# A gated delta rule whose triangular inverse is turned in 32x32 blocks by VectorE, with narrower merge products and K*S in place of W

## The reference

```python
m = jnp.where(strict, jnp.einsum('bhnid,bhnjd->bhnij', kb, k) * decay, 0.0)
t_inv = lax.linalg.triangular_solve(eye + m, ..., lower=True, unit_diagonal=True)
u = jnp.einsum('bhnij,bhnjd->bhnid', t_inv, v * beta[..., None])
w = jnp.einsum('bhnij,bhnjd->bhnid', t_inv, kb * jnp.exp(gc)[..., None])
...
    v_new = u_n - jnp.einsum('bhck,bhkv->bhcv', w_n, state)
    o_n = (jnp.einsum('bhck,bhkv->bhcv', qg_n, state)
           + jnp.einsum('bhij,bhjv->bhiv', qk_n, v_new))
    state = state * jnp.exp(gl_n)[..., None, None] + jnp.einsum('bhck,bhcv->bhkv', kd_n, v_new)
```

## Time and profile before

| | us |
|---|---|
| median of three runs | 3276.89 |
| span of the profiled execution, first to last instruction | 3272.8 |
| TensorE busy (PE) | 3167.1 (97%) |
| VectorE busy (DVE) | 2267.4 (69%) |
| ScalarE busy (ACT) | 1691.8 (52%) |
| GpSimd busy (POOL) | 821.7 (25%) |

### The profile page before, as it was taken

How to read it: one execution, slowest core, us unless ns; L and a number is a source line. 1 busy time by engine, 2 the same in 40 slices (tenths; PEclk the granted TensorE clock), 3 DMA queues, 4 the chain that set the end, 5 groups by cost and what they waited for, 6 DMA issues and landing times.

```text
span 3272.8 us, 62859 instructions
## 1 busy us (share of the span) xinstructions
PE 3167.1 (97%) x19574; PEld 2770.4 (85%) x19574; DVE 2267.4 (69%) x4218; ACT 1691.8 (52%) x3583; POOL 821.7 (25%) x1372
## 2 busy tenths in 40 slices
PE   5999999999989999999999998999999999999998
PEld 4989898989878888888888887888888888888887
DVE  5777777777756588667886767875667645775566
ACT  5565656565644455444555555324555444454444
POOL 1000000000010189888888830661000000000000
PEclk8999999999999999999999999999999999999999
DMA  6444444444447777777777876886666676666754
GB/s 163 120 123 110 129 107 128 112 121 119 116 132 182 202 200 208 210 201 207 200 203 202 209 194 179 239 243 171 181 188 186 179 188 185 180 183 177 182 152 141
DMA packets 1047697, 560.62 MB, mean 171 GB/s; under 512 B 47664, under 2 KB 1035472, under 8 KB 1047104
## 3 DMA queue, kind: packets, MB, share of 16 engines
q1 hardware_dynamic: 980608, 495.38, 56.7%
q10 hardware_dynamic: 58160, 37.63, 4.0%
q0 software_dynamic: 8848, 26.59, 2.6%
HBM read 530.40 MB, written 29.13 MB: 171 GB/s over the span
## 4 chain that ended last, share of the span: by engine, by line
PE 79%; DVE 9%; DMA 4%; issue 4%; ACT 3%; SPq 1%; ACTq 1%; DVEq 0%; POOL 0%; POOLq 0%
PE bank L293 44%; PE bank L294 22%; PE bank L637 5%; DVE w_lo L281 4%; DMA u_scratch<-u 3%; ACT w_hi L275 1%; DVE tiles L1929 1%; DVE normed L1941 1%; PE bank L635 1%; DVE tiles L308 1%; SPq L477 1%; PE bank L698 1%; PE bank L711 0%; PE bank L600 0%; PE bank L751 0%
## 5 line engine op out<-in xcount | busy, mean ns | idle before, releaser
L293 PE MATMUL bank<-act,w_hi 128*128 128x512 f32 x4352 | 1586.3, 406 | 19.6 <-DVE act L330 8.1
L281 DVE TENSOR_TENSOR w_lo<-raw,w_hi 128x512 fp32r<-128x512 f32 x1856 | 1308.2, 755 | 190.6 <-ACT w_hi L275 177.7
L294 PE MATMUL bank<-act,w_lo 128*128 128x256 f32 x4352 | 1217.5, 280 | 0.0
L293 PE MATMUL bank<-mid,w_hi 128*128 128x512 f32 x3072 | 1096.0, 401 | 21.8 <-DVE mid L1943 13.9
L275 ACT ACTIVATE w_hi<-raw 128x512 fp32r<-128x512 f32 x1856 | 1040.2, 621 | 87.1 <-PE bank L294 64.5
L293 PEld LDWEIGHTS bank<-act,w_hi 128*128 128x128 f32 x4352 | 819.8, 188 | 213.5 <-DVE w_lo L281 13.4
L294 PE MATMUL bank<-mid,w_lo 128*128 128x256 f32 x3072 | 865.8, 282 | 0.0
L294 PEld LDWEIGHTS bank<-act,w_lo 128*128 128x128 f32 x4352 | 823.0, 189 | 5.0 <-issue 4.1
L293 PEld LDWEIGHTS bank<-mid,w_hi 128*128 128x128 f32 x3072 | 583.0, 190 | 165.8 <-DVE mid L1943 15.1
L294 PEld LDWEIGHTS bank<-mid,w_lo 128*128 128x128 f32 x3072 | 586.3, 191 | 0.0
L303 ACT ACTIVATE tiles<-bank 128x256 f32<-128x256 f32 x384 | 146.3, 381 | 597.4 <-PE bank L294 593.2
(11 more groups left out here) (325 smaller groups left out, 2945.4 us busy)
## 6 DMA issues: line engine op xcount, KB each, us to landing
raw<-in_mlp_w_up_dram SPq DMA_DIRECT2D x128, 1024.0 KB, 6.4
raw<-in_mlp_w_down_dram SPq DMA_DIRECT2D x128, 1024.0 KB, 6.1
raw<-in_gdn_w_in_dram SPq DMA_DIRECT2D x96, 1024.0 KB, 5.9
raw<-in_gdn_w_out_dram SPq DMA_DIRECT2D x32, 1024.0 KB, 6.5
raw<-in_ple_w_gate_dram SPq DMA_DIRECT2D x32, 1024.0 KB, 6.1
raw<-in_s_w_out_dram SPq DMA_DIRECT2D x28, 1024.0 KB, 6.8
raw<-in_s_w_in_dram ACTq DMA_DIRECT2D x10, 1024.0 KB, 12.6
c_scratch<-c_pow ACTq DMA_DIRECT2D x32, 256.0 KB, 4.4
```

Of the source, the lines that this page charges most:

```text
L281: eng.tensor_tensor(w_lo[par][:, c], raw[slot][:, c], w_hi[par][:, c].bitcast(F32), ALU.subtract).then_inc(S("lo_ready"), 1)
L293: eng.matmul(a[:, :], w_hi[par][:, w], rhs[:, k0 + kt, :], start=(k0 + kt == 0), stop=False)
L294: mm = eng.matmul(a[:, 0:NT], w_lo[par][:, w], rhs[:, k0 + kt, 0:NT], start=False, stop=(k0 + kt == kend - 1))
```

## The change

- VectorE turns Pm, P2, P4 and (in place of all three turns of RT) R, by its transpose of 32x32 blocks; R and the powers are block-diagonal there in blocks of 16 or 32. After the second merge only one 32x32 corner of each half is turned anew. TensorE's turns of Pm and RT and its products for P2T and P4T go, with ScalarE's copies of them.
- P2 is made in slot 0, P4 in slot 1, P8 in slot 2; the products with R follow one slot earlier too, and the first form of R is needed in slot 1.
- The second merge multiplies Mp itself (no L2) by the second half of each pair of columns, 64 moving columns with 96 stationary ones; the third has 64 stationary ones and full 128 rows. ScalarE writes the new columns of RT.
- W and nW go. Vb of block 1 gets minus beta*exp(gc) times K*S added to it (the sign sits in column H_BEXP), by two VectorE operations in slot 12; K*S is one product with 256 columns.
- The state follows one slot earlier. `decays(r+1)` moves from slot 13 to slot 15, ahead of `squares(r+1)`; `scalars(r+1)` moves behind the new operations of slot 12; the slot's `split_lo` goes last there. The rest of VectorE's side work is split in `before` and `after` the core.

TensorE and ScalarE:

```diff
                 if s == 0:
                     w("P_ready")
-                    four(A, Pm, None, "PT_turned", True)
+                    w("PT_ready")
+                    four(C, PT, Pm, "power_done")
                 elif s == 1:
-                    w("power_out", 4, 1)
-                    four(C, PT, Pm, "power_done")
-                    four(F, Pm, PT, "power_done")
-                elif s == 2:
-                    w("power_out", 4, 2)
+                    w("power_out", 3, 1)
                     w("RT_ready", 7, 1)
                     four(A, P2, RT, "R_done")
                     w("transposed_out", 2, 1)
                     four(C, P2T, P2, "power_done")
-                    four(F, P2, P2T, "power_done")
...
+                elif s == 6:
+                    w("RT_ready", 7, 5)
+                    for m in range(4):
+                        mm = pe.matmul(A[0:96, 64 * m:64 * m + 64], Mp[:, m, 0:96], second_half(RT, m), start=True, stop=True)
+                    mm.then_inc(S("X_done"), 1)
                 elif s == 7:
...
+                    for m in range(4):
+                        mm = pe.matmul(C[0:96, 64 * m:64 * m + 64], Dm[:, m, 0:96], packed(WT, m), start=True, stop=True)
...
+                        mm = pe.matmul(A[0:64, 64 * m:64 * m + 64], Mp[:, m, 0:64], RT[:, m, 64:128], start=True, stop=True)
...
+                elif s == 12:
+                    w("sides_ready", 3, 3)
+                    pe.matmul(F[:, 0:NT], kq[:, 1, 1, :], state[:, :, :].rearrange("p h v -> p (h v)"), start=True,
+                              stop=True).then_inc(S("chunk_done"), 1)
                 elif s == 13:
-                    w("sides_ready", 5, 5)
-                    w("sides_ready", 5, 4)
+                    w("Vb_less")
                     for hd in range(2):
-                        dst = A[:, (2 + hd) * P:(3 + hd) * P]
-                        pe.matmul(dst, RT[:, 2 + hd, :], Vb[:, 2 + hd, :], start=True, stop=False)
-                        mm = pe.matmul(dst, nW[:, hd, :], state[:, hd, :], start=False, stop=True)
+                        mm = pe.matmul(A[:, (2 + hd) * P:(3 + hd) * P], RT[:, 2 + hd, :], Vb[:, 2 + hd, :], start=True, stop=True)
...
                 elif s == 13:
-                    decays(r + 1)
                     gate_tanh(n + 6, 0, y[:, 1, :], "conv_done", 4 * r + 6)
                 elif s == 15:
+                    decays(r + 1)
                     squares(r + 1, n + 7)
```

VectorE:

```diff
+                ve.wait_ge(S("P_ready"), r + 1)
+                ve.transpose(fl(PT), fl(Pm)).then_inc(S("PT_ready"), 1)
...
+                if s == 0:
+                    w("power_out", 3, 1)
+                    ve.transpose(fl(P2T), fl(P2)).then_inc(S("transposed_out"), 1)
+                elif s == 1:
+                    add_to_R(1)
+                    w("power_out", 3, 2)
+                    ve.transpose(fl(P4T), fl(P4)).then_inc(S("transposed_out"), 1)
...
+                    add_to_R(3)
+                    w("RT_ready", 7, 4)
+                    ve.transpose(fl(Dm), fl(RT)).then_inc(S("Dm_ready"), 1)
+                elif s == 5:
+                    w("R_done", 6, 4)
+                    w("RT_ready", 7, 4)
+                    TT(fl(RT), fl(RT), C[:, :], ALU.subtract).then_inc(S("RT_ready"), 1)
+                    w("RT_ready", 7, 5)
+                    ve.transpose(fl(Dm), fl(RT)).then_inc(S("Dm_ready"), 1)
+                elif s == 7:
+                    w("RT_ready", 7, 6)
+                    ve.transpose(Dm[32:64, :, 0:32], RT[0:32, :, 32:64]).then_inc(S("Dm_ready"), 1)
...
+                elif s == 12:
+                    w("chunk_done", 5, 3)
+                    w("sides_ready", 3, 2)
+                    for hd in range(2):
+                        last_ = STT(Vb[:, 2 + hd, :], F[:, hd * P:(hd + 1) * P], hs[:, H_BEXP + hd:H_BEXP + hd + 1],
+                                    Vb[:, 2 + hd, :], ALU.mult, ALU.add)
+                    last_.then_inc(S("Vb_less"), 1)
...
-            def around(r, s, last):
+            def before(r, s, last):
 
                 n = 6 * r
-                if s == 1:
+                if s == 0:
+                    ve.wait_ge(S("PT_ready"), r + 1)
+                    TT(RT[:, :, :], PT[:, :, :], ident.unsqueeze(1).to_broadcast([P, 4, P]), ALU.add).then_inc(S("RT_ready"), 1)
+                elif s == 1:
```

More of the change, by code:

```diff
@@ L667, in core @@
                     mm.then_inc(S("qk_done"), 1)
-                elif s == 4:
-                    w("power_out", 4, 4)
+                elif s == 3:
+                    w("power_out", 3, 3)
                     w("RT_ready", 7, 3)
@@ L672, in core @@
                     w("o_log")
-                    for b in range(2):
-                        mm = pe.transpose(E[:, b * P:(b + 1) * P], kq[:, 1, b, :], ident)
-                    mm.then_inc(S("kv_turned"), 1)
-                elif s == 5:
[L677 to L681, removed]
+                    pe.transpose(E[:, 0:P], kq[:, 1, 0, :], ident).then_inc(S("kv_turned"), 1)
+                elif s == 4:
+                    w("RT_ready", 7, 4)
+                    w("L_ready")
+                    four(A, L1, RT, "X_done")
+                elif s == 5:
                     w("Dm_ready", 3, 1)
@@ L718, in core @@
                     mm.then_inc(S("chunk_done"), 1)
[L719 to L723, removed]
+                elif s == 11:
                     w("VN_ready", 2, 1)
-                    w("sides_ready", 5, 2)
                     for hd in range(2):
@@ L1200, in head @@
                             split_hi(se, 6 * r + m, q, m % 3, 2 * r + m // 3 + 1, par=m % 2)
-                    if s in (0, 4, 12, 16, 20):
-                        around(r, s, last)
-                        core(r, s)
-                    else:
-                        core(r, s)
-                        around(r, s, last)
+                    around(r, s, last)
+                    core(r, s)
                     if s == 17:
@@ L1908, in around, with after @@
                     key_matrix(r + 1)
+            def after(r, s):
+                if s == 12:
+                    ve.wait_ge(S("Vb_less"), r + 1)
+                    ve.wait_ge(S("sides_ready"), 3 * r + 3)
+                    scalars(r + 1)
                 elif s == 22:
-                    conv(r + 1, n + 8, 2)
+                    conv(r + 1, 6 * r + 8, 2)
             def head(r, last):
                 for s in range(24):
-                    if s < 8 or not last:
-                        m = 5 + s // 4
-                        split_lo(ve, 6 * r + m, s % 4, 0 if last and m == 6 else m % 3, m % 2)
+                    split = s < 8 or not last
+                    m = 5 + s // 4
+                    quarter = lambda: split_lo(ve, 6 * r + m, s % 4, 0 if last and m == 6 else m % 3, m % 2)
+                    if split and s != 12:
+                        quarter()
                     if s == 19 and not last:
                         unit_qk(r + 1)
+                    before(r, s, last)
                     core(r, s)
-                    around(r, s, last)
+                    if not last:
+                        after(r, s)
+                    if split and s == 12:
+                        quarter()
             with ve.Fori(0, KH - 1) as r:
```

125 lines of the change are left out of this document (44 added, 81 removed).

## The result

| | before | after |
|---|---|---|
| median of 20 runs each, us | 3275.82 (3264.72 to 3293.38) | 3286.97 (3279.82 to 3294.78) |
| span of the profiled execution, us | 3272.8 | 3284.2 |
| TensorE busy, us | 3167.1 | 3113.2 |
| start of the last slot 14, us | 942.56 | 952.38 |

A forecast was written before the change was run, and what follows sets the result against it. TensorE, without idle time in the heads, was taken as the bound. A head of 23.24 + 24.02 + 5.0 + 1.84 = 54.1 us gave -18.2 us in all, lost clock +10, so 3268 us; range 3238 to 3298.

The forecast's parts named there:

- S14 to S1: TensorE's slot 14 to next slot 1 core starts: moved decays and Pm's transpose lengthen R's chain; 23.24 us, 2.9 waiting.
- S11 to S13: TensorE's slot 11 to 13 core starts: VectorE adds K times state to Vb first; 5.0 us, 0.9 waiting.
- S13 to S14: TensorE's slot 13 to 14 core starts: 1.84 us, VectorE reaching the VN copy with some 0.3 to spare.
- S1 to S11: TensorE's slot 1 to 11 core starts: fewer turns and products, narrower weights; 24.02 us, where before it was 29.53.
- I take the share of the loads: Narrow weights on TensorE: a 0.89 us group falls to 0.51 with 64 stationary columns, 0.70 with 96.
- Hidden edits: Other transposed powers, L2's mask, R's transposes, ScalarE's dropped turned copies and the weights' DMA: nothing waited for changes.
- The bounds: Head length for narrow weights gaining nothing to full proportion, and transpose price one to two copies: 53.8 to 55.9 us.
- The clock: Gap at slot 1 drops TensorE's clock to half for 3.4 us: 1.4 us in half of 14 heads, +10 us.
- The ends: Outside the 14 full periods: head 0, with no chain before it, saves 4.3 us; the last one loses 0.8.
- TensorE did not stay the bound: Rival: slack hides both lengthened chains, a head is 49.2 us; 3185 us, chance 0.16 including halfway cases.
- the clock did not hold: Rival: same lengthened chains but no clock loss from the gaps; -18.2 us, 3259 us, chance 0.22.
- it was not lost for longer: Rival: behind slot 1 the clock halves for 6.8 us or falls twice, 2.8 us a head; 3298 us, chance 0.17.

The follow-up runs named there:

- Both experiments on the decays: Changed kernel with decays(r+1) back in ScalarE's slot 13: 3260.7 us, ratio 0.9949; kernel before with decays(r+1) moved to slot 15: 3297.8 us, 1.0065.
- the wide kernel: Changed kernel with all 128 stationary columns in the narrow groups of slots 6 to 9, same moving columns: 3294.7 us, ratio 1.0076 to the kernel before.
- the second scheduling edit: ScalarE's four Vb copies moved from slot 8 to 9, on the changed kernel with decays already back in slot 13: 3260.1 us, ratio 0.9956 to before.
- the Vb copies alone: Changed kernel with only ScalarE's four Vb copies moved from slot 8 to slot 9: 3285.3 us, ratio 1.0033 to the kernel before.
- Nine and four fillers: Unread products in slot 1 ahead of the waits, on the changed kernel with decays and Vb copies moved: nine 3245.7 us (0.9919), four 3239.7 us (0.9889).

## Why the prediction was wrong

Between the spans the change made +11.4 us; the steps gave -8. Both chains that the prediction feared are there, nearly at its prices. What failed is the saving that was to pay for them. By its own terms:

- **S14 to S1: right.** 23.11 us measured (4.77 + 8.88 + 4.61 + 4.85), 23.24 forecast. The turn of Pm, the moved decays and the waits in slots 16 and 1 (1.10 and 2.56 by the starts; 1.1 and 2.9 forecast) are there. Both experiments on the decays show their part.
- **S11 to S13: right,** 4.99 against 5.0, with 0.77 of waiting for Vb against 0.9. S13 to S14 is 1.97 against 1.84.
- **S1 to S11: the step that failed.** It gave 24.02 us, and 25.33 were measured; times 14 that is 18 of the 19 us missed. Two causes are shown. "I take the share of the loads" for the narrow weights credited 1.14 us a head, and the wide kernel says 0.50: of the 0.19 credited for each group of 96 columns 0.18 and 0.10 came, of the 0.38 for each of 64 columns 0.07 and 0.15. The share came from a single load. And the step had no wait in it: the change also moves ScalarE's Vb copies from slot 10 to slot 8, which neither the list of the change nor "Hidden edits" names, and there they push a split and with it the VN copy, 0.47 us. The last 0.2 us are a tenth each in slots 1 and 4, and their cause stays open.
- **The bounds.** With no gain from the narrow weights the sum would have been 55.2 us a head, and its upper bound 55.9 holds the measured 55.40; the forecast time went by the middle term. (The lower bound is 53.9 by its own terms, not 53.8.)
- **The clock: right in kind and price, lucky in the share.** Six of 14 heads, 1.58 us each, 9.5 us; forecast were half of them at 1.4, 10 us. The half was a choice between two gaps with different outcomes, not worked out, and kernels close to this one lose clock in 8, 9, 13 or 14 periods. With no loss in the heads the change would have been +2 and not -18: the waits and the smaller saving give away the gain without it.
- **The ends.** Head 0 came 1.5 us earlier and not 4.3, the last period was 1.6 shorter and not 0.8 longer, and 1.6 us fell behind the heads: together +2.
- **The rivals.** TensorE did not stay the bound, the clock did not hold, and it was not lost for longer than one stretch of 3.4 us a head. The program got slower without any of them: the forecast's own sum was 1.3 us a head too low, on a gain of 1.05.

The Trainium skill ("TensorE: Matmul & The Clock Gate", LDWEIGHTS) has a load's time go with its columns. Here the loads get shorter with fewer columns, but not in proportion (192, 165 and 138 ns), and the starts of the groups, which set the head, gain nothing below 96.

## What to carry to other kernels

When the bound engine loses work, what it gains is set by the first chain through the others that comes up; read each in-order list past its waits, also for copies that only change their slot. Price a narrower instruction by the distance of starts in a group, not by the length of one part of it, and least of all by a single one. Where a gap remains that costs clock, a saving elsewhere may buy nothing until the gap is shortened: four unread products were worth more here than the second scheduling edit.

## What the hardware showed unexpectedly

- Whether a gap costs clock is not told by its length here. With 2.4 us of idle at slot 1, 6 heads of 14 lost it, in the same places in two executions; with the same idle and a head 0.47 us shorter in slot 11, all 14. With 2.13 us, 8 and 13 of 14; with 1.21 us none. What picks the heads among those with a gap stays open.
- In the 14 periods each loss is one stretch of 3.4 us at 0.50. It costs 1.6 us where TensorE is the bound behind it; with the Vb copies alone 1.4 to 1.6, an estimate against the changed kernel's clean head less 0.57.
- A group of eight float32 instructions with 64 moving columns takes 0.81 to 0.84 us from start to next start with 128 stationary columns, 0.62 with 96, 0.61 with 64.
- The part of the program behind the last slot 14 is the same in all kernels and took 2324.4 to 2342.6 us in the profiled executions (2330.2 before, 2331.8 after). This scatter is as large as what several of the edits save. Nine and four fillers have heads of 53.22 and 53.23 us and spans of 3245.4 and 3239.2: 5.0 of the 6.2 us lie behind the heads, 1.0 in the last head. So edits of this size are read from the distance of the slots 14. The +11.4 us of the change itself lie in the heads: +12.9 in the 14 periods.
